# Linear attention with block factors, seven levels for both directions, Q on GpSimd and K on VectorE

## The reference, cut to what matters

```python
b = jnp.cumsum(lc, axis=2)
o_inter = jnp.einsum('bhid,bhde->bhie', qc * jnp.exp(b), S)
diff = b[:, :, :, None, :] - b[:, :, None, :, :]
decay = jnp.exp(jnp.where(mask, diff, -jnp.inf))
A = jnp.einsum('bhid,bhjd,bhijd->bhij', qc, kc, decay)
o = o_inter + jnp.einsum('bhij,bhje->bhie', A, vc)
S_new = jnp.exp(bl[:, :, 0, :, None]) * S + jnp.einsum('bhjd,bhje->bhde', kc * jnp.exp(bl - b), vc)
```

## Time and profile before

| | us |
|---|---|
| median of 3 runs | 3953.41 (3952.99 to 3957.62) |
| span of the profiled execution | 3951.4 |
| what lies around that span, against the median | 2.0 |
| gla0, first to last instruction | 259.0 to 436.1 |
| gla1 | 1395.3 to 1539.3 |

### The profile page before, as it was taken

How to read it: one execution, slowest core, us unless ns; L and a number is a source line. 1 busy time by engine, 2 the same in 40 slices (tenths; PEclk the granted TensorE clock), 3 DMA queues, 4 the chain that set the end, 5 groups by cost and what they waited for, 6 DMA issues and landing times. The chain is left out here.

```text
span 3951.4 us, 57506 instructions
## 1 busy us (share of the span) xinstructions
PE 3497.5 (89%) x22472; PEld 2971.5 (75%) x22472; DVE 2206.5 (56%) x3197; ACT 1271.7 (32%) x1862; POOL 1137.1 (29%) x556
## 2 busy tenths in 40 slices
PE   6978698999998976989996999799999996978998
PEld 3758687888887766878885888677778875757886
DVE  4658553655656465454454788624676665345334
ACT  4123342221222234432233445423343333223222
POOL 3205001322322230134432333233222221424442
PEclk8976798999999967999997999899999998988998
DMA  4430001323322600123321212122111111212231
GB/s 172 152 107 1 1 28 38 112 86 117 118 96 87 209 30 1 33 87 127 133 85 48 68 64 68 60 80 65 39 44 38 46 37 33 90 49 91 96 96 58
DMA packets 85329, 295.27 MB, mean 75 GB/s; under 512 B 13506, under 2 KB 14082, under 8 KB 84740
## 3 DMA queue, kind: packets, MB, share of 16 engines
q1 hardware_dynamic: 84836, 290.74, 22.1%
q10 hardware_dynamic: 288, 1.60, 0.1%
HBM read 290.21 MB, written 2.10 MB: 74 GB/s over the span
## 5 line engine op out<-in xcount | busy, mean ns | idle before, releaser
L245 POOL TENSOR_TENSOR mlp_slab_lo<-slab,mlp_slab_hi 128x1024 fp32r<-128x1024 f32 x144 | 361.2, 2511 | 484.6 <-ACT mlp_slab_hi L226 484.5
L245 POOL TENSOR_TENSOR slab_kept_lo<-slab,slab_kept_hi 128x1024 fp32r<-128x1024 f32 x99 | 243.8, 2463 | 749.5 <-ACT slab_kept_hi L226 749.5
L1949 DVE TENSOR_TENSOR mlp_hid_lo<-mlp_sq,mlp_hid_hi 128x512 fp32r<-128x512 f32 (+1 forms) x96 | 215.2, 2242 | 120.2 <-ACT mlp_hid_hi L1905 119.8
L119 PE MATMUL banks<-mlp_hid_hi,mlp_slab_hi 128*128 128x512 f32 (+1 forms) x768 | 279.6, 364 | 0.0
L120 PE MATMUL banks<-mlp_hid_lo,mlp_slab_hi 128*128 128x512 f32 (+1 forms) x768 | 278.8, 363 | 0.0
L121 PE MATMUL banks<-mlp_hid_hi,mlp_slab_lo 128*128 128x512 f32 (+1 forms) x768 | 278.6, 363 | 0.0
L226 ACT ACTIVATE mlp_slab_hi<-slab 128x1024 fp32r<-128x1024 f32 x144 | 151.5, 1056 | 376.5 <-PE banks L121 331.2
L120 PE MATMUL banks<-hT_mlp_lo,mlp_slab_hi 128*128 128x512 f32 (+1 forms) x576 | 205.2, 356 | 0.0
L119 PE MATMUL banks<-hT_mlp_hi,mlp_slab_hi 128*128 128x512 f32 (+1 forms) x576 | 205.0, 356 | 0.0
L121 PE MATMUL banks<-hT_mlp_hi,mlp_slab_lo 128*128 128x512 f32 (+1 forms) x576 | 204.7, 355 | 0.0
L1946 DVE TENSOR_TENSOR mlp_sq<-mlp_tmp 128x512 f32<-128x512 f32 (+1 forms) x96 | 99.0, 1031 | 178.8 <-ACT mlp_tmp L1900 178.8
(11 more groups left out here) (595 smaller groups left out, 9723.4 us busy)
## 6 DMA issues: line engine op xcount, KB each, us to landing
slab<-in_s_mlp_dram SPq DMA_DIRECT2D x192, 512.0 KB, 3.7
proj_vec_slab<-in_s_vec_proj_dram SPq DMA_DIRECT2D x64, 512.0 KB, 3.6
mlp_vec_slab<-in_s_vec_mlp_dram SPq DMA_DIRECT2D x64, 512.0 KB, 3.6
slab<-in_s_ssm_dram SPq DMA_DIRECT2D x48, 512.0 KB, 3.5
slab<-in_s_gdn_dram SPq DMA_DIRECT2D x48, 512.0 KB, 3.5
slab<-in_s_in_dram SPq DMA_DIRECT2D x32, 512.0 KB, 4.5
slab<-in_s_out_dram SPq DMA_DIRECT2D x24, 512.0 KB, 4.0
slab<-in_s_merge_ssm_dram SPq DMA_DIRECT2D x24, 512.0 KB, 3.5
```

What stands on the lines that cost most here:

```text
L119: nc.tensor.matmul(out, lhs.hi, rhs.hi, start=start, stop=False)
L245: self.nc.gpsimd.tensor_tensor(pair.lo[:], self.raw[u % slots][:], pair.hi[:].bitcast(F32), ALU.subtract).then_inc(self.split, 1)
L1949: nc.vector.tensor_tensor(hid.lo[:, u, :], sq[:, u % 2, :], hid.hi[:, u, :].bitcast(F32), ALU.subtract).then_inc(hid_ready, 1)
```

## The change

The decays are no longer made from running sums by difference and exponential at each level. TensorE sums the gates over blocks of every size at once (c.spans, 256 columns: blocks of 1, 2, 4, ... 128 tokens), ScalarE takes one exponential of these (scale 1/16), and these factors of blocks are multiplied onto Q and K from level to level. Both hold, for each token, the form for pairs within the same direction and the form for the other direction (q_same and q_ways, k_same and k_ways), so that one product of 64 x 64 per head, tile and half holds the entries of both directions. Levels 0 to 5 stay within halves of a tile, level 6 crosses them; D holds the diagonal quarters of A, O the others.

- GpSimd multiplies Q (the pieces of q_same's next buffer, then of q_ways); VectorE does the same for K. ScalarE copies the halves that only change their role (both_turned). Level 6 ends with plain halves.
- VectorE copies entries by mask, 3 times 512 elements a level in gla0 (W = 3), 2 in gla1.
- The rotation of tile 2 stands behind the gates; the scale of the gates is in the exponential.
- The outputs of the blocks come ahead of the states, with accumulation in PSUM; norm and gate are done per pair of tiles, out of PSUM; the gate's silu stands at the start of the levels.
- The constants have spans, joins and sides in place of 14 masks (1730 columns for 2562), and gdn reads its masks from them directly.

```diff
-    c.mask_f = c.const[:, 6 * P:13 * P].rearrange("p (m f) -> p m f", m=LEVELS)
-    c.mask_b = c.const[:, 13 * P:20 * P].rearrange("p (m f) -> p m f", m=LEVELS)
+    c.spans = c.const[:, 5 * P:7 * P]
+    c.joins = c.const[:, 7 * P:10 * P].rearrange("p (m f) -> p m f", f=64)
+    c.sides = c.const[:, 10 * P:13 * P].rearrange("p (m f) -> p m f", f=64)
...
+        def pieces(out, x, t0, lev, which, at, by):
+
+            m, n = 1 << lev, C - t0
+            at_x, by_x = (0, 3 * m) if which == 0 else (m, m)
+            for pr in (None,) if t0 == 0 else range(2):
+                tiles = 2 * n if pr is None else n
+                start = t0 * P + (pr or 0) * TOK
+                f_start = ((pr or 0) * C + t0) * 512 + 2 * SPAN_AT[lev] + at
+                for sl in range(1 if m in (1, 32) else 2):
+                    if m == 1:
+                        dims, f = [(4, tiles * 32), (by_x, 2)], [(512, tiles), (8, 32), (by, 2)]
+                    elif m == 32:
+                        dims, f = [(P, tiles), (by_x, 2), (1, m)], [(512, tiles), (by, 2), (0, m)]
+                    else:
+                        dims, f = [(4 * m, tiles * (32 // m)), (1, m)], [(512, tiles), (8, 32 // m), (0, m)]
+                    yield (spread(out, dims, start + at_x + sl * by_x), spread(x, dims, start + at_x + sl * by_x),
+                           spread(spans[:], f, f_start + sl * by))
...
+                pe.wait_ge(moved, U + 1)
                 for t in range(C):
                     pe.wait_ge(la_ready, t + 2)
+                    for pr in range(2):
...
+                        for d in range(2):
+                            last = nc.tensor.matmul(c.ps[:, 6 + t % 2 if pr else t, 256 * d:256 * d + 256], la[:, t, (2 * d + pr) * P:(2 * d + pr + 1) * P],
+                                                    c.spans, start=True, stop=True)
+                        last.then_inc(t_full, 1)
+
+                def sibling_products(K, Q, across, w, done):
+
+                    for e in range(4):
+                        t, pr = first + 2 * w + e // 2, e % 2
+                        for kb in range(2):
+                            for h in range(2):
+                                r, k0, q0 = slice(64 * h, 64 * h + 64), t * P + 64 * kb, t * P + 64 * (1 - kb if across else kb)
+                                last = nc.tensor.matmul(c.ps[64 * kb:64 * kb + 64, 2 * w + h, 64 * e:64 * e + 64],
+                                                        K[r, pr, k0:k0 + 64], Q[r, pr, q0:q0 + 64], start=True, stop=True)
+                    last.then_inc(done, 1)
...
+                for lev in range(LEVELS):
+                    if lev:
+                        pe.wait_ge(q_next, lev + 1)
+                        pe.wait_ge(q_moved, lev + 1)
+                        pe.wait_ge(k_next, lev + 1)
+                        pe.wait_ge(k_moved, lev + 1)
...
+                    for w in range(W):
+                        pe.wait_ge(a_read, lev * W + w + 2)
+                        sibling_products(k_same[lev % 2], q_same[lev % 2], lev == TOP, w, a_full)
+                    if lev in (1, 3):
+                        pool_mix(lev // 2)
+
+                pe.wait_ge(top_read, W + 1)
...
+                for n, t in enumerate(o_order):
+                    for qb in range(2):
+                        for h in range(GLA_H):
+                            nc.tensor.matmul(out_at(t, 64 * h, 64)[64 * qb:64 * qb + 64], entry(O if qb else D, t, h // 2, h % 2),
+                                             c.tok[:, t, C_GV + 64 * h:C_GV + 64 * h + 64], start=n % 2 == 0 and h == 0, stop=False, skip_group_check=True)
...
+                nc.scalar.activation(k_ways, c.gqk[:, 2:4, :], ACT.Copy).then_inc(k_copied, 1)
...
             def _(pool):
-                        lo, hi = b_[:, pr, :, 0:m], b_[:, pr, :, m:2 * m]
-                        ref = b_[:, pr, :, edge:edge + 1].to_broadcast(list(lo.shape))
...
+                pool.wait_ge(q_begun, 5)
+                for lev in range(TOP):
+                    same, other_ = q_same[lev % 2], q_same[(lev + 1) % 2]
...
+                    for out, x_, f in pieces(other_, same, first, lev, 0, 3, 1):
+                        last = nc.gpsimd.tensor_tensor(out, x_, f, ALU.mult)
+                    last.then_inc(q_next, 1)
+                    pool.wait_ge(q_moved, lev + 2)
+                    for out, x_, f in pieces(q_ways, same, first, lev, 1, 0, 7):
+                        last = nc.gpsimd.tensor_tensor(out, x_, f, ALU.mult)
+                    last.then_inc(q_turned, 1)
...
+                for lev in range(TOP):
...
+                    for out, x_, f in pieces(other_, same, 0, lev, 0, 2, 3):
+                        last = nc.vector.tensor_tensor(out, x_, f, ALU.mult)
+                    last.then_inc(k_next, 1)
+                    mask = c.sides[:, lev, :].bitcast(U32).unsqueeze(1).unsqueeze(1).to_broadcast([P, 2, 4, 64])
+                    for w in range(W):
...
+                        nc.vector.copy_predicated(entries(D, w), mask, wave(w)).then_inc(a_read, 1)
+                    dve.wait_ge(k_moved, lev + 2)
+                    for out, x_, f in pieces(k_ways, same, 0, lev, 1, 1, 5):
+                        last = nc.vector.tensor_tensor(out, x_, f, ALU.mult)
+                    last.then_inc(k_turned, 1)
```

More of the change, by code:

```diff
@@ L960, in projection, with spread @@
     ring.close()
+def spread(x, dims, at=0):
+    return bass.AP(x.tensor, x.offset + at, [x.ap[0]] + [list(d) for d in dims])
+SPAN_AT = [0, 128, 192, 224, 240, 248, 252, 254]
 def gla(c, name, l, a, first):
@@ L968, in gla @@
     s0 = first * P
-    nb = C - first
-    parts = [(t, min(4, C - t)) for t in range(first, C, 4)]
-    M = len(parts)
+    W = (C - first) // 2
+    TOP = LEVELS - 1
     with Stage(c, name) as st:
@@ L1000, in gla @@
[L1000 to L1005 removed]
+        other = more[:].rearrange("p (x a n) -> p x a n", x=4, a=2)
@@ new lines, in _ @@
+                pe.wait_ge(q_turned, TOP + 2)
+                pe.wait_ge(q_moved, TOP + 2)
+                for t in o_order:
+                    at_of_d = [order(d).index(t) for d in range(2)]
+                    pe.wait_ge(s_ready, max(at_of_d) + 1)
+                    terms = [(q_same[1] if d == 0 else q_ways, at - 1, d) for d, at in enumerate(at_of_d) if at]
+                    for p_ in range(2):
+                        for e, (q, at, d) in enumerate(terms):
+                            last = nc.tensor.matmul(out_at(t, p_ * P, P), q[:, p_, t * P:(t + 1) * P], S[:, at, 2 * d + p_, :], start=False,
+                                                    stop=e == len(terms) - 1, skip_group_check=True)
@@ L1187, in _ @@
-                act.wait_ge(a_full, 2 * LEVELS * M + 1)
-                nc.scalar.activation(qd[:], bT[:], ACT.Exp).then_inc(decays, 1)
-                for t in range(C):
-                    for dp in range(4):
-                        col = t * P + last_col[dp // 2]
-                        last = nc.scalar.activation(kd[:, dp, t * P:(t + 1) * P], bT[:, dp, t * P:(t + 1) * P], ACT.Exp,
-                                                    scale=-1.0, bias=bT[:, dp, col:col + 1])
-                    last.then_inc(decays, 1)
@@ L1195, in _ @@
-                for d in range(2):
-                    bl = bT[:, 2 * d:2 * d + 2, :].rearrange("p d (t f) -> p d t f", f=P)[:, :, :, last_col[d]]
-                    nc.scalar.activation(ebl[:, 2 * d:2 * d + 2, :], bl, ACT.Exp).then_inc(decays, 1)
+                    for pr in range(2):
+                        act.wait_ge(t_full, 2 * t + pr + 2)
+                        nc.scalar.activation(spread(spans[:], [(1, 2), (2, 256)], (pr * C + t) * 512),
+                                             c.ps[:, 6 + t % 2 if pr else t, :].rearrange("p (s n) -> p s n", s=2), ACT.Exp, scale=1.0 / 16).then_inc(t_exp, 1)
@@ new lines, in _ @@
+                for pr in range(2):
+                    q = c.gqk[:, pr, s0:].rearrange("p (n s) -> p n s", s=2)
+                    for out, at, by in ((q_same[0], 1, 1), (q_ways, 0, 3)):
+                        f = spread(spans[:], [(512, C - first), (4, 64), (by, 2)], (pr * C + first) * 512 + at)
+                        nc.vector.tensor_tensor(out[:, pr, s0:].rearrange("p (t n s) -> p t n s", t=C - first, s=2),
+                                                q.rearrange("p (t n) s -> p t n s", t=C - first), f, ALU.mult).then_inc(q_begun, 1)
@@ L1355, in _ @@
[L1355 to L1356 removed]
+                    last.then_inc(s_ready, 1)
+                for n in range(len(o_pairs)):
+                    dve.wait_ge(o_sq, n + 2)
+                    nc.vector.tensor_reduce(st_[:, 0, 4 * first + 8 * n:4 * first + 8 * n + 8], sq[:, n * 512:n * 512 + 512].rearrange("p (n e) -> p n e", e=64),
+                                            AX, ALU.add).then_inc(gated, 1)
```

380 lines of the change are left out of this document (183 added, 197 removed).

## The result

The changed kernel takes 3861.6 us (median of four runs, 3860.2 to 3863.5) beside 3953.2 for the kernel before (four runs, 3947.8 to 3957.6): a ratio of 0.9765, 95% interval 0.9751 to 0.9779. The span of its profiled execution is 3859.8 us, before 3951.4: 91.6 us shorter. The forecast was 3879 with a range of 3853 to 3913, and 74.3 us off the span. The size of the gain, not its sign, was off: 17.3 us more than forecast. Stage gla0 is 58.3 us shorter than before and gla1 36.4; the levels of layer 0, 14 before and 7 now, fell from 75.1 to 31.9 us.

The account below looks back on a forecast made before the run. TensorE at half clock and GpSimd and VectorE in turn were all close to the bound in the levels. Span 3951.4 - 44.6 (gla0) - 28.7 (gla1) - 1.0 (constants) = 3877.1, median 2.0 above: 3879 us, range 3853 to 3913.

Parts of the forecast that it names:

- wide array: Rival (chance 0.2): four array quarters run at once, pass 2.6 us; total 3868 us, or 3853 with exclusion hardly binding.
- Fewer levels, about the same price per level: Levels of gla0 and gla1: three engines near the bound, only fewer levels help; layer 0 goes from 14 to 7.
- GpSimd and VectorE in turn: Levels: the two engines' pieces exclude each other, summing to 5.3 us a level in layer 0, 5.1 or 4.4 in layer 1.
- TensorE in the levels: Layer 0 levels: 96 instructions, 5.1 us at half clock, set the order; 7 passes plus pool products make 41.3 us.
- pool products: Layer 0 levels: two pool products lie in TensorE's order, 2.8 us each with the wait around them.
- To the first level: Factors ready to first level product: 10.2 us in layer 0, 7.1 in layer 1; 96 same-token products 2.8 to 5.1.
- Head: Stage start to factors: products 12.8 us, rotation moved behind gates; layer 0 factors ready at 300.8, 1.1 us later than before.
- Level in layer 1: GpSimd's eight 128-element pieces, 0.39 us each, in turn with VectorE make 5.1 us, 4.4 at two levels; levels end 1474.5.
- Tail: Last level product to stage end: 39.2 us in layer 0, 36.1 in layer 1; block outputs ahead of states counted as gain.
- Constants: Kernel start: constants shrink from 2562 to 1730 columns, 0.43 MB; 1.1 us, of which 1.0 is taken as gain.
- dear pieces: Rival (chance 0.07): GpSimd multiplications by factors with repeats cost twice 0.83 us in the levels; total 3907 us.
- cold clock: Rival (chance 0.2): all head and tail products run at 1.2 GHz, giving 32.7 us back; total 3912 us.

Follow-up runs that it names:

- yardsticks: The changed kernel run again unaltered, twice, as reference for the other follow-up kernels of its group: after_again_b 3858.9 us and after_third 3861.1 us.
- transposes_by_wave_b: Changed kernel, but TensorE's transposes of turned keys wait for their own wave's three corner copies, not all nine: 3857.0 us, 0.9738 of the kernel before.
- all_four: Changed kernel plus transposes waiting by wave, VectorE sharing Q's turned pieces from level two, block outputs after state products, first-wave corner copies earlier: 3846.0 us.
- after_third: The changed kernel repeated without edits as reference for the last group: 3861.1 us, 0.9751 of the kernel before.
- after_again_b: The changed kernel repeated without edits as reference for the second group: 3858.9 us, 0.9741 of the kernel before.

## Why the forecast was right, and where it was off

The forecast was right in the direction and in the main cause: half as many levels at about the same price each. Its account of what sets a level in layer 0 was wrong. That the number still lies in the range is due to the rival of the wide array (chance 0.2), for which the range was kept open. Each part in turn:

- **Fewer levels, about the same price per level.** Right: 7 levels at a period near that of one of the 14 before (5.8 us then, 5.1 to 5.6 now once the second level is past), and both stages shorter. GpSimd and VectorE in turn, which the forecast priced and then set aside for TensorE, set the period; its sum of 5.3 us is near what was measured, with prices of GpSimd that were too low.
- **TensorE in the levels.** This step failed: "TensorE: 96 instructions, 5.1 us at half clock" and "TensorE then sets the order". The spacing of 0.029 us in the stage of the gated delta rule was read at full clock, rightly (the granted clock of these products is 1.00); but it was doubled, and taken over to another order of quarters. Measured are 0.017 at full and 0.030 at half clock. It made the levels of layer 0 41.3 us; they took 31.9. Of the 17.3 us by which the forecast missed, this one is 9.4. The price of the pass was less decisive than it looks: even at 0.040 an instruction the levels are only 34.4 us. The exclusion was the bound in layer 0, and the pool products, counted as 5.6 us of their own, lie in TensorE's idle time.
- **To the first level.** 6.7 and 5.3 us in place of 10.2 and 7.1: the same price again (96 same-token products in 1.63 us and not 5.1).
- **Head.** 41.1 and 41.3 us in place of 41.8 and 41.5: right, the products at 12.29 us in both layers too. Of its reasons, the moved rotation holds in layer 0 alone. The 41.1 of layer 0 was 42.2 in one of the two yardsticks.
- **Level in layer 1.** Right in kind: GpSimd's small pieces set it. Left alone by VectorE, four pieces of 128 take 1.52 us at spans of 16 tokens, 0.38 each, as the 0.39 of the forecast; the others take 1.9 to 3.2 us beside VectorE, the first 3.9. The levels took 27.7 us, 30.6 forecast: half of the difference is TensorE's last pass, 2.0 us and not 3.4.
- **Tail.** 39.0 us and 39.2 forecast in layer 0, but by errors that cancel, so this hit is luck: TensorE waits 7.4 us behind the last pass and not 3.8, with the corner copies ending last (transposes_by_wave_b, where they no longer do, still waits 3.8 us for VectorE's last half); block outputs took 4.1 and not 5.8, last outputs some 4 and not 5.6. One reason was wrong in sign: block outputs ahead of the states cost 5 to 7 us in layer 0 and 3 to 5 in layer 1. In layer 1 the tail took 33.3 us, 36.1 forecast.
- **Constants.** At the start 0.9 us were gained (mod starts at 12.8 and not at 13.7), but gla0 begins at 259.0 as before. In the thirteen profiles with this start it begins anywhere from 256.7 to 263.4, so whether the forecast's 1.0 us came through can't be read.
- **Rivals.** The wide array (3868, or 3853 without exclusion) is the nearest. Its mechanism holds in that four quarters overlap, and in that exclusion and VectorE set the levels; its price for layer 0 (7.8 more) was 9.4. The dear pieces showed in part: some 2 us at the first level, and at the second 1.18 us for a piece of 384 and not 0.83. The argument against them, that pieces at all strides take the same 0.83, was a misreading: in the kernel before, with VectorE idle, one of the two kinds of pieces took 1.00 us at blocks of 4 tokens and 0.91 at blocks of 8 (lines below, the timeline of GpSimd). A cold clock did not come: the factor products of both heads took 12.29 us and not 20.6, with a clock of 0.86, and the tail of gla0 had 0.80.

```profile
343.95 1.00 POOL L1228 TENSOR_TENSOR gla_r<-gla_bT 128x384 f32<-128x384 f32 x1 [0.89 <-DVE gla_qd L1299]
344.90 0.83 POOL L1229 TENSOR_TENSOR gla_r<-gla_bT 128x384 f32<-128x384 f32 x1
...
350.52 0.91 POOL L1228 TENSOR_TENSOR gla_r<-gla_bT 128x384 f32<-128x384 f32 x1 [3.05 <-DVE gla_qd L1299]
```

Of the 17.3 us, 13.7 come from gla0 (0.7 head, 3.5 to the first product, 9.4 levels, 0.2 tail) and 7.7 from gla1 (0.2, 1.8, 2.9 and 2.8). Against them stand the 1.0 of the constants and 3.1 elsewhere; the stage of the gated delta rule alone is 3.5 us longer (655.1 us and not 651.6). That was not the change: the same code took 651.5 to 651.8 us in eight other executions, 652.9 in one and 655.1 to 656.8 in three. So the masks read from the constants cost nothing that can be seen.

## What to carry to other kernels

Before pricing a stage by its busiest engine, add up what two engines that exclude each other do in turn: here that sum lay within 10% of the period of 5.1 to 5.3 us, while the price of TensorE's pass could go from 1.6 to 3.8 us and lengthen the levels of layer 0 by 1.4 to 2.5 us only. Price strided or broken-up pieces from rows with the same pattern. A pattern of small products has to be priced by rows with the same order of quarters at the same clock, not by doubling another's. After the large gain look at what idles in the chain that is left: 15 us more, a sixth of the whole gain, came from the order of two blocks of products, three copies and a semaphore's threshold, and from giving VectorE the small pieces.

## What the hardware showed unexpectedly

- The granted clock in the levels of layer 0 did not follow how busy TensorE was. With the same products in three orders it was 0.79 (busy 19.1 of 32.1 us), 0.78 (22.9 of 33.2) and 0.95 (30.5 of 34.4); but in all_four it was 0.93 with only 16.5 of 30.3 us busy, and in after_third, the changed kernel itself, 0.73 (20.0 of 33.0).
- The 3.4 us of the stage of the gated delta rule lie in one chain of products near its end. The table by stretches for the same work, in the profile after and then in after_again_b:

```profile
3134.00:3154.00 20.00, 17.11 (x116) 14.62 (x115) 11.20 (x23) 2.30 (x4) 2.36 (x1) 0.74 0.01 3
```

```profile
3132.40:3148.90 16.50, 14.15 (x115) 12.32 (x112) 8.83 (x23) 2.30 (x4) 2.39 (x1) 0.90 0.01 3
```

The same 115 instructions take 17.1 and 14.2 us, at a clock of 0.74 and 0.90: time multiplied by clock is 12.7 us in both. transposes_by_wave_b lost its 3.4 us at the same place; the other two long executions lost most of theirs between 108 and 223 us into the stage. Where the low clock falls differs between executions of one program, and is worth 3.4 us here.
